# The second block's input projection, recurrence and half of its output projection, handed out between the attention heads' products

## What is computed

```python
def second_block(x, ...):
    h = rmsnorm(x, norm1_g)
    proj = h @ w_in                      # 1024 -> 2560
    xa, ya, sq, sk, sv, dq, dk, dv = jnp.split(proj, split_at, axis=-1)
    xa = causal_dwconv(xa, conv_a_w, conv_a_b)
    out_a = rg_lru(xa, ...) * jax.nn.gelu(ya)          # 512 channels: a gated linear recurrence
    out_b = stick_breaking(heads(sq), heads(sk), heads(sv))        # 4 heads of 64
    out_c = diff_attention(heads(dq), heads(dk), heads(dv), ...)   # 4 heads, two score maps each
    mixed = jnp.concatenate([out_a, out_b, out_c], axis=-1)        # 1024 channels
    x = x + mixed @ w_out
    ...
# stick_breaking, for keys s earlier than the query t:
#   weights = exp(log_sigmoid(z) + sum over later keys of log_sigmoid(-z)),  out = weights @ v
# diff_attention: out = (softmax(q1 k1) - lam * softmax(q2 k2)) @ v, then an rmsnorm per head
```

## Time and profile before

| what | us |
|---|---|
| median of 3 runs | 2149.15 |
| runs | 2145.08 to 2149.46 |
| the profiled execution's own time | 2152.7 |
| its span in the trace | 2150.9 |
| TensorE busy | 1988.2 |
| VectorE busy | 1268.7 |
| ScalarE busy | 884.5 |

### The profile page before, as it was taken

How to read it: one execution, slowest core, us unless ns; L and a number is a source line. 1 busy time by engine, 2 the same in 40 slices (tenths; PEclk the granted TensorE clock), 3 DMA queues, 4 the chain that set the end, 5 groups by cost and what they waited for, 6 DMA issues and landing times.

```text
span 2150.9 us, 43896 instructions
## 1 busy us (share of the span) xinstructions
PE 1988.2 (92%) x19070; PEld 1535.4 (71%) x19070; DVE 1268.7 (59%) x1955; ACT 884.5 (41%) x1333; POOL 99.5 (5%) x122
## 2 busy tenths in 40 slices
PE   5999799999999998599999999999977799999997
PEld 3677576766667666488888888887863378888885
DVE  5562267777777777444555555546545647777532
ACT  3242245546455464433222222444445445444321
POOL 2000000000000000000000000001121100000000
PEclk8999999999999999799999999999987699999998
DMA  3224311111101110133322322232200022222331
GB/s 118 73 79 134 108 43 37 36 38 40 43 30 38 43 39 8 66 122 107 98 98 98 98 98 94 93 98 89 69 30 1 0 69 91 96 98 98 91 98 66
DMA packets 49293, 154.54 MB, mean 72 GB/s; under 512 B 8272, under 2 KB 10576, under 8 KB 48592
## 3 DMA queue, kind: packets, MB, share of 16 engines
q1 hardware_dynamic: 48960, 149.65, 21.5%
q10 hardware_dynamic: 144, 2.10, 0.3%
HBM read 145.43 MB, written 6.29 MB: 71 GB/s over the span
## 4 chain that ended last, share of the span: by engine, by line
PE 52%; DVE 4%; ACT 1%; issue 0%; DMA 0%; ACTq 0%; DVEq 0%
PE bank L1368 15%; PE bank L1367 15%; PE bank L1369 15%; PE bank L1482 1%; PE bank L1428 1%; PE bank L1427 1%; PE bank L1426 1%; PE bank L1462 1%; DVE tmp L1862 0%; PE bank L1489 0%; PE bank L1456 0%; DVE tmp L1997 0%; PE bank L1465 0%; PE bank L1411 0%; DVE tmp L1942 0%; DVE zone L1971 0%
## 5 line engine op out<-in xcount | busy, mean ns | idle before, releaser
L1524 ACT ACTIVATE w_hi<-raw 128x1024 fp32r<-128x1024 f32 (+1 forms) x192 | 201.7, 1051 | 573.9 <-PE bank L1369 521.5
L1367 PE MATMUL bank<-h_hi,w_hi 128*128 128x512 f32 x992 | 389.4, 393 | 0.0
L1368 PE MATMUL bank<-h_lo,w_hi 128*128 128x512 f32 x992 | 386.4, 390 | 0.0
L1369 PE MATMUL bank<-h_hi,w_lo 128*128 128x512 f32 x992 | 386.3, 389 | 0.0
L148 DVE TENSOR_TENSOR w_lo<-raw,w_hi 128x1024 fp32r<-128x1024 f32 (+1 forms) x192 | 232.9, 1214 | 167.6 <-ACT w_hi L1524 167.5
L1367 PEld LDWEIGHTS bank<-h_hi,w_hi 128*128 128x128 f32 x992 | 186.6, 188 | 40.4 <-issue 1.6
L1368 PEld LDWEIGHTS bank<-h_lo,w_hi 128*128 128x128 f32 x992 | 186.5, 188 | 40.3 <-issue 1.7
L1369 PEld LDWEIGHTS bank<-h_hi,w_lo 128*128 128x128 f32 x992 | 186.5, 188 | 38.7
L141 PE MATMUL bank<-xg_hi,g_hi 128*128 128x512 f32 x256 | 104.9, 410 | 25.2 <-DVE xg_lo L148 17.1
L1367 PE MATMUL bank<-y_hi,w_hi 128*128 128x512 f32 x256 | 101.8, 398 | 12.8 <-DVE y_lo L148 12.8
L670 ACT ACTIVATE swapT<-invT 64x256 f32<-64x256 f32 x160 | 66.4, 415 | 106.7 <-DVE invT L1128 57.5
(11 more groups left out here) (345 smaller groups left out, 4087.0 us busy)
## 6 DMA issues: line engine op xcount, KB each, us to landing
raw<-in_w_conv SPq DMA_DIRECT2D x64, 512.0 KB, 3.2
raw<-in_w_up SPq DMA_DIRECT2D x44, 512.0 KB, 3.3
raw<-in_w_out SPq DMA_DIRECT2D x40, 512.0 KB, 3.7
raw<-in_w_in SPq DMA_DIRECT2D x20, 512.0 KB, 3.3
g_raw<-in_w_g SPq DMA_DIRECT2D x16, 512.0 KB, 3.4
g_raw<-in_w_r SPq DMA_DIRECT2D x16, 512.0 KB, 3.8
w_k<-in_w_k SPq DMA_DIRECT2D x16, 512.0 KB, 3.5
w_v<-in_w_v SPq DMA_DIRECT2D x16, 512.0 KB, 3.7
```

What stands on the lines that cost most here:

```text
L1367: pe.matmul(to, whi, hi, start=begin, stop=False)
L1368: pe.matmul(to, whi, lo, start=False, stop=False)
L1369: last = pe.matmul(to, wlo, hi, start=False, stop=end)
L1524: act.activation(w_hi[:, g % RING, 0:width], raw[:, g % RAW, 0:width], ACT.Copy).then_inc(S("whi"), 1)
```

## The change

The stages `in_stage` and `attention` are folded together. `in_stage` keeps only four units (`HEAD`: the first chunk each of both kinds' queries and keys). The other sixteen units, the eight gate products and half of the output projection (for each of its 8 chunks the four products with channels that are ready early) become `ITEMS`. A generator, `between()`, hands them to TensorE in slots: a slot is three products of 512 columns (or twelve of 128 for the values, or one gate product). `STEPS` says for each head how many slots come after each of nine places in the head: at its start, after each of the four score blocks, after the tail, after the transposes, and after each product with the values. VectorE and ScalarE get the evacuations, splits and parts of the recurrence in `behind(n, s)`, at the same nine places, when an item has ended in that place. Two banks (5 and 7) take the items in turn, so an item waits for the evacuation of the one before the last. The z scores of a head are packed into one stretch of 1280 columns over three banks and treated in one instruction where there were four; the two maps of the other scores share one instruction; what GpSimd added and scaled for the attention moves to VectorE or falls away; the last value product is cut into ten of 128 columns. The buffers are laid out anew for all this (one `room` for the old `first`, `extra`, `tmp` and part of `zone`). The output stage keeps the other four chunk products of each unit. The core of the diff:

```diff
-    stage("in2", [ins["w_in2"][k] for k in range(20)])
-    stage("out3", cut(ins["w_out3"], DC))
+    HEAD = [8, 10, 12, 14]
+    ITEMS = [("v", 0), ("v", 2), ("x", 0), ("y", 0), ("x", 1), ("g", 0), ("y", 1), ("q", 9), ("q", 11), ("q", 13),
+             ("g", 1), ("q", 15), ("x", 2), ("y", 2), ("x", 3), ("g", 2), ("y", 3), ("v", 1), ("v", 3), ("g", 3)]
+    ITEMS += [("o", n) for n in range(DC)]
+    LRU_AT = {3: [(0, 0)], 5: [(0, 1)], 6: [(0, 2)], 7: [(0, 3)], 8: [(1, 0)], 10: [(1, 1)], 11: [(1, 2)], 12: [(1, 3)],
+              13: [(2, 0)], 15: [(2, 1)], 16: [(2, 2)], 17: [(2, 3), (3, 0)], 19: [(3, 1), (3, 2), (3, 3)]}
+    STEPS = [(4, 2, 3, 4, 9, 5, 5, 5, 5), (4, 2, 3, 4, 9, 5, 5, 5, 5), (6, 4, 4, 6, 11, 6, 5, 8, 2),
+             (0, 0, 0, 4, 8, 4, 4, 4, 8)]
+    LONG = {"v": 8, "q": 8, "x": 8, "y": 8, "g": 2, "o": 4}
...
+            def between():
+                for i, (kind, n) in enumerate(ITEMS):
+                    for q in range(2 if kind == "g" else 1):
+                        t = turn_of(i) + q
+                        to = bank[BANK[t % 2]]
...
+                        if t >= 2:
+                            pe.wait_ge(S(turns[t - 2][0]), turns[t - 2][1])
...
             def attention():
...
+                scores(0)
                 for n in range(4):
+                    fill(n, 0)
...
                     for b in range(TB):
...
+                        t.then_inc(S("d_mm"), 1)
+                        fill(n, 1 + b)
+                    pe.wait_ge(S("spm"), 2 * n + 2)
...
+                    t.then_inc(S("tail_mm"), 1)
+                    fill(n, 5)
...
                         t.then_inc(S("pT_mm"), 1)
+                    fill(n, 6)
+                    if n < 3:
+                        scores(n + 1)
...
                     t.then_inc(S("sb_mm"), 1)
+                    fill(n, 7)
...
                     t.then_inc(S("do_mm"), 1)
+                    fill(n, 8)
...
+            def behind(n, s_):
+                for i in ended(n, s_):
+                    kind, number = ITEMS[i]
...
+                    if kind != "g":
+                        split(unit_of(i) + RING)
+                    for n_, part_ in LRU_AT.get(i, []):
+                        lru(n_, part_)
+                    if i < 6:
+                        residual(2 + i)
+                    if (kind, number) == ("g", 3):
+                        for k in range(6):
+                            part(k)
...
+                            dve.scalar_tensor_tensor(out=sp_, in0=zs, scalar=0.0, in1=za, op0=ALU.max, op1=ALU.add)\
+                                .then_inc(S("sp"), 1)
+                            dve.wait_ge(S("sp"), n + 1)
+                            need(dve, S("sb_mm"), n)
+                            dve.tensor_tensor(ex, zs, sp_, ALU.subtract).then_inc(S("logw"), 1)
...
+                    dve.wait_ge(S("tail_mm"), n + 1)
+                    dve.tensor_tensor(ex, ex, zs, ALU.add).then_inc(S("sum"), 1)
+                    behind(n, 5)
```

More of the change, by code:

```diff
@@ L1430, in in_stage @@
+            def in_stage():
+                for k in range(4):
+                    unit(AT["in2"] + k, bank[k][:, :], of(h), range(DC), True, True, "h2_lo" if k == 0 else None)
                     if k == 0:
                         totals("out2")
[L1432 to L1446 removed]
+                pe.wait_ge(S("copied"), 4)
```

491 lines of the change are left out of this document (263 added, 228 removed).

## The result

The changed kernel takes 2187.05 us (median of 4, 2184.87 to 2188.23), the kernel before 2149.31 beside it. The ratio is 1.0175, with a 95% interval of 1.0155 to 1.0195: it is slower by some 38 us. The forecast was 2157, 8 us slower, with a range up to 2176. The direction was right, the size was not.

The account below looks back on a forecast made before the run. It took a chain of TensorE and VectorE taking turns in attention as the bound. Work 226.1, waits 73.2 and clock 20.3 gave 319.6 us against 311.4, 8.2 slower: about 2157 us, range 2118 to 2176.

Parts of the forecast that it names:

- I count 2.5 us for each of the waits of over 3.5 us that comes amid work: Clock loss over the four heads: 2.5, 4.8, 5.1, and 7.9 for the fourth, which starts cold; sum 20.3 us.
- TensorE's work: TensorE's work at full clock from the fourth input-projection unit to the output projection's last addition: 226.1 us.
- the stretch: From the fourth input-projection unit's evacuation to the output projection's last addition: 311.4 us before, 319.6 forecast.
- The waits: TensorE's idle time over the four heads, the gap before the fourth and the output projection: 73.2 us.
- at the transposes: TensorE waits there while VectorE does an item's work: 6.4, 9.2, 4.7 and 5.8 us by head, 26.1 in all.
- between the third and fourth head: The recurrence's whole last chunk runs there with nothing beside it: 16.3 us of waiting.
- clearly less than 70 us: Sign that the forecast is wrong: TensorE's waits in the stretch come to clearly less than 70 us.
- the line through the pieces: VectorE's packed instruction of 1280 columns takes 1.49 us, read from shorter pieces, against 1.94 for the four before.
- 0.8 more on the chain, four times: Behind each head's tail the whole packed 1.49 us now follows, where only 0.69 did: 3.2 us in all.
- The slots cover: Rival: the transposes' waits (26.1 us) and the clock falls behind them (10.2) don't come about, kernel at 2121; chance 0.30.
- The clock stays low: Rival: the clock stays low from the third head's end, 15 us on top, kernel at 2172; chance 0.15.
- It cancels: Rival: single waits are 4 to 10 us shorter in all, no difference can be measured; chance 0.13.

Follow-up runs that it names:

- dense_12: Changed kernel plus 12 unread 512-column products at each of two entries to value slots (first and third head): 2163.55 us, ratio 1.0065.
- all_ahead: Changed kernel with all 20 handed-out projection and gate items run ahead of attention, packed heads kept: 2179.89 us, ratio 1.0158.
- all_ahead_b2: all_ahead with VectorE's work that hangs on the logarithm moved from behind the first to behind the third score block: 2169.55 us, ratio 1.0102.
- v_block: Changed kernel with the first head's value slots in one piece, ahead of its first small score product: 2190.61 us, ratio 1.0194.
- before_light: Kernel before, with four 64-row products and the eight one-column products put ahead of its value units: 2175.19 us, ratio 1.0132.
- all_ahead_busy: all_ahead_b2 plus unread 512-column products in TensorE's waits in the first three heads: 2150.11 us, ratio 1.002.
- v_ahead_b2: Changed kernel with v0 and v2 as a block ahead of the first scores, VectorE's logarithm work behind the third score block: 2167.22 us, ratio 1.0091.
- x_first: Changed kernel with item x0 (512-column products) handed out ahead of value items v0 and v2: 2186.61, 2168.24, 2166.70 and 2189.29 us, ratio 1.0118.

## Why the prediction was wrong in size

- **The term that failed is the clock.** The step "I count 2.5 us for each of the waits of over 3.5 us that comes amid work" gave 20.3; 57.1 were lost. No row had shown a bound of 3.5 us, and none of the runs does. Two things in the step were wrong. The fall needed no long wait: in the first head it came after 0.88 us of idle time and light products. And the price was set by what ran afterwards, not by the wait: 27.8 us in the first head against 2.5 counted, 15.9 in the third against 5.1. Where no value slots follow, the step was about right: 7.1 against 4.8, and 6.4 against 7.9. The prediction had value units at 1.00 in its rows and took it for granted that they run so wherever they stand. dense_12 shows that this term explains most of the miss: with 25.5 us lost, near the 20.3 forecast, the kernel stands 15 us above the one before, of which 5.5 are the added products. That the 9 to 10 that remain lie by the 8.2 of the forecast is in part luck: in that run the waits are 11.6 less than forecast, TensorE's work without the added products 8.5 more and the clock 5.2 more.
- **The kernel before already showed such a fall.** The last value unit there ends at 1586.2. Then come 0.78 us of idle time and light score products, and the clock is at 0.50 from 1590 on (the earlier trace rows begins there). Nearly the same entry now stands ahead of v0:

```profile
1587.02 2.42 PE L1445 MATMUL bank<-first 64*128 64x512 f32 x8 [0.78 <-DVE gate L1923]
```

```profile
1589.00:1590.00 1.00, 0.86 (x8) 0.52 (x6) 0.11 (x1) 0.98 (x3) 0.00 (x0) 0.95 0.31 82
```

- **The working of that step was loose as well.** By its own list the second head has one wait of over 3.5 us (9.2; the others are 2.3, 3.3 and 2.8), not two. Half of the 6.0 us of the earlier trace rows is 3.0, not 2.5. The 7.9 of the fourth head has no working. This moves the term by a few us, the value slots by 36.
- **The direction was right by the clock, not by the mechanism forecast.** With the measured work (232.8) and waits (61.0) and the forecast's own 20.3 for the clock, the stretch would be 314.1 us against 312.0 before: less than a measurement tells from none.
- **The waits** came in the places named, nearly all of them somewhat shorter: at the transposes 5.1, 7.8, 3.2 and 4.5 us against 6.4, 9.2, 4.7 and 5.8, in sum 20.6 for 26.1; at the third head's third block 6.5 against 7.1; between the third and fourth head 14.6 against 16.3. At the fourth head's third block it was longer, 5.6 against 4.5. In all 61.0 idle for 73.2. By the mark that I had set ("clearly less than 70 us") the waits were overcounted, by a sixth. Between the third and fourth head two pieces were overcounted: GpSimd's step, 1.98 us and not 2.45, and the six low parts, 3.7 and not 4.5 (the earlier trace rows has four in 2.49, which is 0.62 each and not 0.75).
- **TensorE's work** was 6.7 us too low (226.1 for 232.8). Of that, 3.6 lie in the rest of the output projection, where 20.3 were forecast and 23.9 are busy; the prediction's own 5.6 us a unit gives 22.4 for eight halves.
- **The packing.** The 1280 columns took 1.49 us, as the line through the pieces said. But "0.8 more on the chain, four times" saw only the tail's side; heads without slots came 4.7 and 6.0 us later than before (all_ahead), and 10 us in all went with the place of the block. How much of the rest is packing no run shows. Within the changed kernel this lies in the waits at the score blocks, which the walk did count. Of the rule of the Trainium skill that stood beside this step (Perfetto Trace Analysis, Optimizing Scalar/DVE Operations), all_ahead shows the condition of the second half: VectorE was not saturated, and its packed work held TensorE up by 7.3 us. No run breaks that work up; all_ahead_b2 only moves it.
- **The rivals.** "The slots cover": no, the transposes waited 20.6 us. "The clock stays low" was the right idea in the wrong place: the fourth head had 0.83 and lost 6.4, the first head was where it stayed low. "It cancels": no, the 38 us are clear of noise.

Not settled: what else holds all_ahead_b2 22 us above the kernel before. Its first finished block comes 5.8 us later than before (1619.33 for 1613.53), though its fourth unit is evacuated 2.3 us earlier (1460.52 for 1462.85), and its second head takes 5.4 us more (41.0 for 35.6); no run took these apart. Nor is it shown what in the light entries brings the clock down, and why it does so in some executions only.

## What to carry to other kernels

Read the granted clock beside TensorE's busy share for every piece of work that you move: a piece that ran at full clock behind dense products may run at half behind light ones, and then it costs as much again. Before moving it, look at what TensorE does in the microseconds ahead of its new place, and keep small products from leading a long run of narrow ones. Where an engine has unavoidable short waits, products that nobody reads can be worth more than the waits' removal: here they gave 10 us for a few lines, while the reordering cost 38. And take several executions: a kernel can have two times that lie 20 us apart.

## What was not expected of the hardware

- Value products (128 columns each) without a gap stayed at 0.50 for 38 us (v_block), 36 (before_light and all_ahead_busy) and 37 (v_ahead_b2). In the kernel before, the same products with one pair of gate products among them stayed at 1.00 for 42 us. At half clock they stayed to the end of the block; where the clock fell, it did so 0.9 us (the changed kernel) to 4 us (x_first) after the first of them. The Trainium skill (TensorE: Matmul & The Clock Gate, Part 1) says that sustained matmul activity releases the throttle; in these windows TensorE was busy throughout, and the clock stayed at 0.50.
- The same program entered such a block at either level from one execution to the next: x_first 2167 and 2168 against 2187 and 2189, v_ahead_b2 2165 to 2169 against 2188, all_ahead_busy 2144 to 2152 against 2164 to 2166. The profiles show the low level in one execution of each, and the granted clock of the whole execution is lower in each of the slower ones (0.949 against 0.958 and 0.961; 0.951 against 0.959 to 0.961; 0.964 to 0.966 against 0.971 to 0.974). A median over few executions of such a kernel says little; the profile of one does not show that the other exists.
- 5.5 us of added products took 23.5 us off (dense_12).
